# Second attention of the second mixer: scores of query groups 1 to 3 from high and low parts

## The reference, cut to what matters

```python
qr = apply_rope(q, cos, sin)
ks = apply_rope(k_slc, cos, sin)
kw = apply_rope(k_win, cos, sin)
s = jnp.einsum('bqgjd,bqgnld->bqgjnl', qb, kg).astype(jnp.float32) * scale   # selected
s = jnp.einsum('bqgjd,bkgd->bqgjk', qb, kb).astype(jnp.float32) * scale      # window
p = jax.nn.softmax(s, axis=-1)
o = g[..., 0:1] * o_cmp + g[..., 1:2] * o_slc + g[..., 2:3] * o_win
```

## Time and profile before

| | |
|---|---|
| median of 3 runs | 2190.43 us (2189.98 to 2190.97) |
| time of the profiled execution | 2189.99 us |
| its span in the profile | 2187.6 us |
| TensorE busy | 2162.0 us, 99% of the span |
| VectorE busy | 1135.8 us, 52% |
| ScalarE busy | 902.9 us, 41% |
| granted TensorE clock, mean | 0.999 of full |

### The profile page before, as it was taken

One profiled execution on the slowest core, in us unless ns is written; L12 is line 12 of the kernel. 1 busy time (PEld: TensorE's weight loads), 2 busy tenths in 40 slices (PEclk: granted clock), 3 DMA queues, 4 the chain that ended last, 5 costly groups with the idle time before them and its releaser, 6 DMA issues.

```text
span 2187.6 us, 28277 instructions
## 1 busy us (share of the span) xinstructions
PE 2162.0 (99%) x11532; PEld 1777.5 (81%) x11532; DVE 1135.8 (52%) x1984; ACT 902.9 (41%) x1525; POOL 0.2 (0%) x4
## 2 busy tenths in 40 slices
PE   8999999999999999999999999999999999999999
PEld 5888988888888888888887878887777888888887
DVE  4664663443433454344356677746776354434344
ACT  5654545442322332222234466546666233222224
POOL 0000000000000000000000000000000000000000
PEclk9999999999999999999999999999999999999999
DMA  5121522123323222323223532321111322332321
GB/s 185 59 78 59 177 98 73 44 92 102 99 90 106 90 93 96 102 92 104 90 94 98 172 99 80 99 83 49 41 34 40 96 95 86 99 98 98 103 87 68
DMA packets 190034, 199.45 MB, mean 91 GB/s; under 512 B 7745, under 2 KB 185042, under 8 KB 189394
## 3 DMA queue, kind: packets, MB, share of 16 engines
q1 hardware_dynamic: 189906, 197.66, 28.1%
HBM read 188.73 MB, written 2.10 MB: 87 GB/s over the span
## 4 chain that ended last, share of the span: by engine, by line
PE 96%; DVE 2%; ACT 1%; issue 1%; DMA 0%; SPq 0%; DVEq 0%; ACTq 0%
PE lin L539 27%; PE lin L541 27%; PE lin L540 27%; PE turned L636 3%; PE score L731 3%; PE mix L745 2%; PE mix L1146 1%; PE mix L992 1%; PE score L972 1%; PE score L822 1%; DMA raw<-in_w_in_dram 0%; DVE arena L2054 0%; PE score L1191 0%; PE mix L1199 0%; PE score L956 0%
## 5 line engine op out<-in xcount | busy, mean ns | idle before, releaser
L539 PE MATMUL lin<-xh,wh 128*128 128x512 f32 (+1 forms) x1478 | 581.7, 394 | 2.6 <-issue 1.9
L541 PE MATMUL lin<-xh,wl 128*128 128x512 f32 (+1 forms) x1478 | 568.9, 385 | 0.0
L540 PE MATMUL lin<-xl,wh 128*128 128x512 f32 (+1 forms) x1478 | 567.6, 384 | 0.0
L539 PE MATMUL lin<-ah,wh 128*128 128x512 f32 x1044 | 407.9, 391 | 0.5 <-DVE h L2096 0.5
L541 PE MATMUL lin<-ah,wl 128*128 128x512 f32 x1044 | 405.5, 388 | 0.0
L540 PE MATMUL lin<-al,wh 128*128 128x512 f32 x1044 | 405.4, 388 | 0.0
L2035 DVE TENSOR_TENSOR wl<-raw,wh 128x2048 fp32r<-128x2048 f32 x130 | 298.0, 2292 | 190.8 <-ACT wh L1303 190.8
L1303 ACT ACTIVATE wh<-raw 128x2048 fp32r<-128x2048 f32 x130 | 247.8, 1906 | 265.5 <-PE lin L541 263.6
L539 PEld LDWEIGHTS lin<-xh,wh 128*128 128x128 f32 x1478 | 277.9, 188 | 64.1 <-issue 12.2
L541 PEld LDWEIGHTS lin<-xh,wl 128*128 128x128 f32 x1478 | 277.7, 188 | 56.6
L540 PEld LDWEIGHTS lin<-xl,wh 128*128 128x128 f32 x1478 | 278.2, 188 | 52.3 <-issue 1.0
(11 more groups left out here) (327 smaller groups left out, 2118.4 us busy)
## 6 DMA issues: line engine op xcount, KB each, us to landing
raw<-in_ffn_w_dram SPq DMA_DIRECT2D x60, 1024.0 KB, 5.1
raw<-in_w_in_dram SPq DMA_DIRECT2D x39, 1024.0 KB, 5.1
raw<-in_mlp_w_dram SPq DMA_DIRECT2D x32, 1024.0 KB, 5.5
raw<-in_xattn_wkv_dram SPq DMA_DIRECT2D x8, 1024.0 KB, 5.4
raw<-in_w_out_dram SPq DMA_DIRECT2D x8, 1024.0 KB, 5.1
arena<-arena SPq DMA_DIRECT2D x104, 64.0 KB, 2.1
raw<-in_ffn_w_dram SPq DMA_DIRECT2D x8, 768.0 KB, 4.5
raw<-in_xattn_wq_dram SPq DMA_DIRECT2D x4, 1024.0 KB, 5.1
```

Of the source, the lines that this page charges most:

```text
L539: nc.tensor.matmul(o, w[0], x[0], start=first, stop=False)
L540: nc.tensor.matmul(o, w[0], x[1], start=False, stop=False)
L541: return nc.tensor.matmul(o, w[1], x[0], start=False, stop=last)
```

## The change

In query groups 1 to 3 a score is now formed from fp32r parts. The high parts of the two heads' queries stay in their row half, and the low part of each goes to the other half: tile `2*it+pr` of `ah` holds head 0's high part above its low part, the same tile of `al` holds head 1's low part above its high part. As the keys are the same in both halves, one matmul over all 128 rows against the high part of the keys gives high x high plus low x high. A second matmul on the 64 rows of the high queries adds high x low from the low part of the keys. A piece is thus: 128 rows for head 0, 128 rows for head 1, 64 rows for head 0, 64 rows for head 1. Group 0 stays as it was.

New on ScalarE are `key_high` and `query_high` (16 copies to fp32r, 4 of 128x512 and 12 of 64x512), new on VectorE `key_low` and `query_low` (16 subtractions of the same shapes), put into the hand-written order at `nq2`, `ga1`, `nq3` and `ga2`. The parts of the keys of group 0 use tiles 6 and 7 of `ah` and `al`, those of group 1 the place of `S_kd` itself. New semaphores tie them: `ky_hi`, `ky_lo`, `qs_hi`, `qs_lo`. The rotation of the queries of group 3 no longer waits for the scores of group 1.

```diff
+                        if n == 0:
+                            pe.wait_ge(ky_lo, 2 * g + 2)
+                        pe.wait_ge(qs_lo, 4 * it - 2 + 2 * pieces[-1][1])
+                        for e, (br, pr, t, col) in enumerate(pieces):
+                            nk, tok = (t + 1) * PART, slice(t * PART, (t + 1) * PART)
+                            both = [x[:, 2 * it + pr, tok] for x in (ah, al)]
+                            for a in range(2):
+                                nc.tensor.matmul(ps[a][:, col:col + nk], both[a], K_h[g][:, br, 0:nk], start=True, stop=False)
+                            for a in range(2):
+                                r = slice(a * HALF, (a + 1) * HALF)
+                                mm = nc.tensor.matmul(ps[a][:, col:col + nk], both[a][r], K_l[g][r, br, 0:nk], start=False, stop=True)
...
+            def key_high(g):
...
+                for br in range(2):
+                    nc.scalar.activation(K_h[g][:, br, :], S_kd[:, br, g, :], ACT.Copy).then_inc(ky_hi, 1)
+            def query_high(it, pr):
...
+                for a, x in enumerate((ah, al)):
+                    r = slice(a * HALF, (a + 1) * HALF)
+                    nc.scalar.activation(x[r, 2 * it + pr, :], S_q[it % 2][r, pr, :], ACT.Copy).then_inc(qs_hi, 1)
...
+                    elif it == 2 and n == 0:
+                        key_high(0)
+                        query_high(1, 0)
...
-                if it >= 2:
+                if it == 2:
                     for a in range(2):
-                        dve.wait_ge(at_s[a], U0["ns"] + (it - 1) * NG_NS)
+                        dve.wait_ge(at_s[a], U0["ns"] + NG_NS)
...
+            def query_low(it, pr):
+                for a, x in enumerate((ah, al)):
+                    r, other = slice(a * HALF, (a + 1) * HALF), slice((1 - a) * HALF, (2 - a) * HALF)
+                    dve.wait_ge(qs_hi, 4 * it - 4 + 2 * pr + a + 1)
+                    low(x[other, 2 * it + pr, :], S_q[it % 2][r, pr, :], x[r, 2 * it + pr, :], qs_lo)
```

More of the change, by code:

```diff
@@ L282, in build @@
         kd = sem("kd")
+        ky_hi, ky_lo, qs_hi, qs_lo = sem("ky_hi"), sem("ky_lo"), sem("qs_hi"), sem("qs_lo")
         vt_t, vt_c, ht_s, cs_r, gt_t, gt_c = sem("vt_t"), sem("vt_c"), sem("ht_s"), sem("cs_r"), sem("gt_t"), sem("gt_c")
@@ L378, in build @@
         S_mg = A(KT, T)
+        S_kp = Arena(att_end, arena_r)(2, 2, T)
+        K_h = [ah[:, 6:8, :], S_kp[:, :, 0, :]]
+        K_l = [al[:, 6:8, :], S_kp[:, :, 1, :]]
         assert A.at <= AW, A.at
@@ L1202, in compressed, with pair @@
                     return dict(scores=scores, mix=mix, turn=[(pr, lo, lo) for pr in range(2) for lo in (0, PART)], read=2 * it + 2)
-                def pair(it, pieces, first):
+                def pair(it, n, pieces):
                     g = it // 2
                     def scores():
[L1208 to L1211, removed]
+                        if it == 0:
+                            if n == 0:
+                                pe.wait_ge(rp_d, R0["ns"] + 2)
+                            causal_scores(pieces, lambda pc, a, tok: S_q[it % 2][a * HALF:(a + 1) * HALF, pc[1], tok],
+                                          lambda pc, a, nk: S_kd[a * HALF:(a + 1) * HALF, pc[0], g, 0:nk])
+                            return
+                        if n == 0:
+                            pe.wait_ge(ky_lo, 2 * g + 2)
[8 more added lines that the diff above has]
+                                mm = nc.tensor.matmul(ps[a][:, col:col + nk], both[a][r], K_l[g][r, br, 0:nk], start=False, stop=True)
+                                if e == len(pieces) - 1:
+                                    mm.then_inc(at_s[a], 1)
                     def mix():
@@ L1219, in ns @@
                 for it in range(4):
-                    pgs += [compressed(it)] + [pair(it, pieces, n == 0) for n, pieces in enumerate(NS_PAIRS)]
+                    pgs += [compressed(it)] + [pair(it, n, pieces) for n, pieces in enumerate(NS_PAIRS)]
                 yield from attend(U0["ns"], pgs, 4 * NG_NS + 3)
@@ L1911, in _ @@
             hidden(1)
+            def key_high(g):
+                if g:
+                    for a in range(2):
+                        act.wait_ge(at_s[a], U0["ns"] + NG_NS)
+                else:
+                    act.wait_ge(lin_done, 2 * P["wda3"] + 2)
+                for br in range(2):
+                    nc.scalar.activation(K_h[g][:, br, :], S_kd[:, br, g, :], ACT.Copy).then_inc(ky_hi, 1)
+            def query_high(it, pr):
+                act.wait_ge(rp_d, R0["ns"] + 2 * it + pr + 1)
+                if it == 3:
+                    for a in range(2):
+                        act.wait_ge(at_s[a], U0["ns"] + 2 * NG_NS)
+                for a, x in enumerate((ah, al)):
+                    r = slice(a * HALF, (a + 1) * HALF)
+                    nc.scalar.activation(x[r, 2 * it + pr, :], S_q[it % 2][r, pr, :], ACT.Copy).then_inc(qs_hi, 1)
             def nq_panel(it, parts=2):
@@ L1928, in nq_panel @@
                     yield
+                    if it == 2 and n == 0:
+                        query_high(1, 1)
+                    elif it >= 2 and n == 2:
+                        query_high(it, 0)
                 evac(p, 1, S_qr[:, 1, :])
@@ L1937, in ga_panel @@
                         yield
+                        if i in (1, 2) and c == 0 and n == 2:
+                            query_high(i + 1, 1)
+                        elif i == 1 and c == 1 and n == 0:
+                            key_high(1)
                     hi(p + 2, c)
@@ L2739, in rope_ns, with key_low @@
                     dve.wait_ge(at_o, U0["da"] + 3 * NC)
-                if it >= 2:
+                if it == 2:
                     for a in range(2):
-                        dve.wait_ge(at_s[a], U0["ns"] + (it - 1) * NG_NS)
+                        dve.wait_ge(at_s[a], U0["ns"] + NG_NS)
                 rope(R0["ns"] + 2 * it + c, S_q[it % 2][:, c, :], S_qr[:, c, :], S_sg[:, c, :])
+            def key_low(g):
+                for br in range(2):
+                    dve.wait_ge(ky_hi, 2 * g + br + 1)
+                    low(K_l[g][:, br, :], S_kd[:, br, g, :], K_h[g][:, br, :], ky_lo)
+            def query_low(it, pr):
[3 more added lines that the diff above has]
+                    low(x[other, 2 * it + pr, :], S_q[it % 2][r, pr, :], x[r, 2 * it + pr, :], qs_lo)
             def nq_panel(it, parts=2):
@@ L2755, in nq_panel @@
                         rope_ns(1, 1)
+                    elif n == 2 and it == 2:
+                        key_low(0)
+                        query_low(1, 0)
+                    elif n == 6 and it == 2:
+                        query_low(1, 1)
+                    elif n == 7 and it == 3:
+                        query_low(3, 0)
                     elif n == 1 and it == 3:
@@ L2780, in ga_panel @@
                             rope_ns(before[i], 1)
+                        elif i == 1 and (c, n) == (0, 2):
+                            query_low(2, 0)
+                        elif i == 1 and (c, n) == (1, 1):
+                            query_low(2, 1)
+                        elif i == 1 and (c, n) == (1, 2):
+                            key_low(1)
+                        elif i == 2 and (c, n) == (0, 3):
+                            query_low(3, 1)
                     if i in before:
```

## The result

The changed kernel takes 2198.87 us (median of 6 runs, 2198.18 to 2200.22), the kernel before 2190.34 us beside it (6 runs). The ratio is 1.0039, 95% interval 1.003 to 1.0049: 8.5 us slower, where 10.1 were forecast. The profiled execution took 2198.18 us, its span is 2196.0 us, 8.4 more than before, at a mean granted clock of 1.000 of full (0.999 before).

What follows compares the result with a forecast made beforehand. TensorE was taken to bound the kernel. +9.8 us of longer score steps, +0.9 and +0.5 of late copies, -1.1 swallowed by waits gave +10.1 on 2189.99, thus 2200.1, with the median 2200.5 us; 8-in-10 range 2194.0 to 2205.0.

Steps and rivals of the forecast that it cites:

- TensorE's stream goes into the end one for one: Whole kernel: TensorE busy 2162.0 of 2187.6 us, so changes to its stream reach the end time in full.
- A change of shape costs 0.20 us: TensorE, switching between 128 rows and row halves: 0.20 us each, about half before the new shape's first matmul.
- The bounds, 0.10 and 0.30: Limits for one change of the array's shape on TensorE, in us; 6.3 us down and up in the total.
- 512 keys +0.03, 256 and 256 +0.45, 128 and 384 +0.61: Added us per score step of groups 1 to 3, by keys per piece: to 1.09, 1.52 and 1.68 us.
- the first block's 1.35 us: First block's step with 128 and 384 keys (109.81 to 111.16), from which the forecast derived the new step's 1.68 us.
- One change less behind the compressed branch: The 256 and 256 step after the compressed value product now begins with 128 rows too: -0.20 us per query group.
- Late copies: 0.9 and 0.5 us: TensorE waits 0.9 us for ScalarE's first four copies near 1513, 0.5 for VectorE's last subtractions near 1633 us.
- Waits that swallow part of it, 1.1 us: Existing TensorE waits for ScalarE and VectorE behind the score steps absorb some of their added time: -1.1 us.
- Rival B: Next shape's weights load during the last matmul, so changes cost nothing: about -0.5 us, 2190.0; chance 0.07.
- C: Rival: a change of shape costs half, 0.10 us; 2194.7 us in all; chance 0.07.
- D: Rival: 0.30 us a change in short runs, or copies pushing each other back in more cycles; 2206.8 us; chance 0.06.

Runs made afterwards that it cites:

- e3: Against the changed kernel: in two-piece score steps all matmuls over 128 rows come first, then those on row halves, one change of shape inside; 2194.89 us.
- e2: Against the changed kernel: all copies, subtractions and their semaphore waits stay, but groups 1 to 3 are scored by the earlier float32 matmuls; 2193.73 us.
- e7: Against the changed kernel: four of the inserted pieces of ScalarE and VectorE work moved to idle time, matmuls untouched; 2198.27 us.
- e4: Against the changed kernel: score matmuls grouped by shape, those on row halves first and those over 128 rows last; 2191.76 us.
- e5: Against the changed kernel: low parts of keys also multiplied over all 128 rows, four such matmuls a piece, none on row halves; 2192.61 us.
- e1: Against the changed kernel: each piece is three pairs of matmuls on row halves, same copies, no change of shape inside a step; 2191.45 us.
- e6: Against the changed kernel: pieces as three pairs on row halves (e1), and four inserted pieces of ScalarE and VectorE work moved to idle time; 2188.22 us.

## Why the prediction was right, point by point

- **TensorE's stream goes into the end one for one.** Busy time +8.4, span +8.4 us. That both agree to 0.1 is partly chance: waits in the attention grew by 0.7, and idle time elsewhere fell by as much.
- **A change of shape costs 0.20 us, read off the first block.** Right for 512 columns: 0.10 before the first matmul of the new shape and 0.10 in it, in the changed kernel as in the earlier trace rows. For a 128-column matmul it was too much. 1531.63 to 1531.84 is 0.21, a 128-column step (0.11) plus 0.10; but from there to 1532.09, 0.25, is that step, 0.10 for leaving again and only 0.05 for having come. 0.15 in all. Around 384 columns it is 0.20 again (1532.37 to 1532.63, 0.26, and 1532.63 to 1533.01, 0.38, at 0.17 a step), and around 256 (e3). The mean of all is 0.18, below. The bounds, 0.10 and 0.30, held it. The Trainium skill's rule that a change of tiling mode drains the engine ("TensorEngine Tiling (Array Packing)", Key Properties) was the right one to weigh against this change; the trace agrees, with 0.10 us before the first matmul of the new shape, and adds that about as much again (0.05 to 0.10) goes into the first load.
- **512 keys +0.03, 256 and 256 +0.45, 128 and 384 +0.61.** Measured +0.04, +0.43 (+0.40 behind the compressed branch) and +0.48. The last is the term that was mis-sized, 12 x 0.13 = 1.6 us, and this is nearly the whole difference between 10.1 and 8.5. That it is so is luck in part: the waits came out 0.4 us above the forecast, and 0.4 us were lost outside the attention. Two things account for 0.11 of the 0.13: the short change (0.05), and the 0.06 us that a 384-column matmul takes longer behind a 128-column one of the same shape. That one was in the first block's 1.35 us and was carried over, but in the changed kernel a change of shape stands between the two.
- **One change less behind the compressed branch.** -0.20 forecast; the time from that value product to the scores went from 1.87 to 1.71 us, -0.16, three times.
- **Late copies: 0.9 and 0.5 us.** The same two places waited, 0.65 and 0.43 us longer than before. The first was forecast from four copies in 2.61 us; these four took 2.34 (1512.04 to 1514.38). The second was right by luck: the forecast left the longer scores out of it, and e2, without them, shows 0.9, half of which they cover. A third was missed: behind the blocks of group 2's second half TensorE lost 0.4 us near 1567 (0.29 of it the wait for VectorE at 1568.27), where the forecast had counted on the longer scores to hide them. In e7, with these blocks moved, this wait is gone.
- **Waits that swallow part of it, 1.1 us.** In TensorE's timeline 0.31 us around the value product at 1615.58 of the kernel before, and 0.48 ahead of that at 1654.87 (its wait was 0.96 and is 0.50), 0.8 in all. Together with the late ones +0.7, forecast +0.3.
- **Rival B** (a change costs nothing): excluded by each of e3, e4 and e5, and by the rows. **C** (0.10): 0.15 to 0.20 is above it. **D** (0.30): they are below it, and the copies didn't cascade. From the steps: the changed kernel's stream is 8.2 us longer, e1's without any change of shape inside a step 2.9 us shorter (12 x 0.15 + 6 x 0.16 + 12 x 0.01), so 63 changes cost 11.1 us, 0.18 each.

The attention groups' steps add up: 12 x 0.48 + 6 x 0.42 + 9 x 0.04 - 3 x 0.16 + 0.7 = 8.9 us. The profiled executions show 8.8 (8.1 in the stretch, 0.65 ahead of it), and the span 8.4; the 0.4 us between lies outside the attention and was not followed up.

## What to carry to other kernels

Count the changes of the array's shape in a stream of short matmuls before counting columns: here one costs as much as 330 to 450 columns of fp32r (0.15 to 0.20 us, at 0.23 for 512). Merging two products into one over all 128 rows won nothing here, even without the changes: a pair of matmuls on the two row halves costs one step, so three products of two heads are three steps as three pairs (e1), and two matmuls over 128 rows with one pair are three steps as well. The 2.9 us that the new form saves on TensorE are all there in e1; no merged form (e3, e4, e5) came out below it. Where shapes have to be mixed, put all matmuls of one shape together, and end with the shape of what follows. Work put on an idle engine costs what the first instruction behind it is late, so it goes where that engine waits anyway (e6, e7), and a slower step beside it can hide that price until the step is mended.

## What the runs showed of the hardware that was not expected

- A change of shape costs 0.15 us between 128-column matmuls, and 0.20 us around 256, 384 and 512 columns.
- The weights of the first matmul of a new shape start to load only with that matmul (1542.14), those of the next one 0.23 us ahead of it at 512 columns (1541.58).
- An fp32r matmul of 384 columns that follows one of 128 columns in the same shape starts the next one 0.23 us later, not 0.17 (e3 at 1533.25, e5 at 1532.50). No run tells why.
- A ScalarE copy of 64 partitions by 512 takes as long (0.63 us) as one of 128 partitions (0.62). The two copies to the two row halves start 0.65 us apart (1513.08, 1513.73), the two of 128 partitions ahead of them 0.52 (1512.04 and 1513.08 are two apart). Why isn't shown: the four copies of 128 partitions in the earlier trace rows, each behind a wait of its own, are 0.66 us apart too.
